# Inverse transforms of a Hyena group, split into even and odd tokens, with the halves of the spectrum summed and subtracted by GpSimd

## The reference, cut to what matters

```
v, x1, x2 = split(short_conv_centred(u))
z = x1 * fft_long_conv(v, k_freq[:, 0], skip[0])
z = x2 * fft_long_conv(z, k_freq[:, 1], skip[1])
return rmsnorm(z, norm_w)

def fft_long_conv(u, k_freq, d):          # u: (B, L, W), L = 256
    y = irfft(rfft(u, n=2 * L) * k_freq, n=2 * L)[:, :L]
    return y + u * d
```

## Time and profile before

| | us |
|---|---|
| median of 3 runs (1463.59 to 1465.66) | 1464.34 |
| the profiled execution's own time | 1464.21 |
| its span, first to last instruction | 1462.4 |
| TensorE busy in it | 1389.9 (95%) |
| GpSimd busy in it | 689.5 (47%) |

### The profile page before, as it was taken

One profiled execution on the slowest core, in us unless ns is written; L12 is line 12 of the kernel. 1 busy time (PEld: TensorE's weight loads), 2 busy tenths in 40 slices (PEclk: granted clock), 3 DMA queues, 4 the chain that ended last, 5 costly groups with the idle time before them and its releaser, 6 DMA issues.

```text
span 1462.4 us, 16428 instructions
## 1 busy us (share of the span) xinstructions
PE 1389.9 (95%) x6832; PEld 1098.3 (75%) x6832; DVE 462.2 (32%) x657; ACT 479.9 (33%) x730; POOL 689.5 (47%) x423
## 2 busy tenths in 40 slices
PE   5879999999899999999999899999989999999997
PEld 2567777787688877888876778777868888888885
DVE  3477754533302311000054677554250000000003
ACT  0764323323333222321247343312442322322212
POOL 0266544344455544544332756533625555555441
PEclk9989999999899999999999999999999999999999
DMA  4322111012333322333312211111213323323331
GB/s 172 105 61 70 44 44 44 30 52 78 117 94 98 91 85 87 115 97 90 101 46 84 72 44 56 38 38 44 72 62 97 102 88 99 101 95 112 96 96 77
DMA packets 31465, 116.82 MB, mean 80 GB/s; under 512 B 3488, under 2 KB 3616, under 8 KB 31136
## 3 DMA queue, kind: packets, MB, share of 16 engines
q1 hardware_dynamic: 31392, 115.78, 25.1%
HBM read 113.67 MB, written 2.10 MB: 79 GB/s over the span
## 4 chain that ended last, share of the span: by engine, by line
PE 83%; DVE 11%; ACT 3%; issue 1%; POOL 1%; DMA 0%; POOLq 0%; DVEq 0%; SPq 0%; ACTq 0%
PE ps L998 16%; PE ps L1000 15%; PE ps L999 15%; PE ps L1005 7%; PE ps L1006 7%; PE ps L1008 7%; PE ps L1195 4%; PE ps L1181 3%; PE ps L1118 2%; DVE amat L852 1%; PE ps L1045 1%; PE ps L1143 1%; DVE ring L836 1%; DVE cum L816 1%; POOL w_lo L641 1%
## 5 line engine op out<-in xcount | busy, mean ns | idle before, releaser
L641 POOL TENSOR_TENSOR w_lo<-w_raw,w_hi 128x1024 fp32r<-128x1024 f32 x198 | 475.1, 2400 | 533.0 <-ACT w_hi L362 533.0
L998 PE MATMUL ps<-h_hi,w_hi 128*128 128x512 f32 x1104 | 450.7, 408 | 3.1 <-POOL w_lo L641 1.6
L1000 PE MATMUL ps<-h_hi,w_lo 128*128 128x512 f32 x1104 | 433.2, 392 | 0.0
L999 PE MATMUL ps<-h_lo,w_hi 128*128 128x512 f32 x1104 | 432.9, 392 | 0.0
L362 ACT ACTIVATE w_hi<-w_raw 128x1024 fp32r<-128x1024 f32 x198 | 208.1, 1051 | 206.6 <-PE ps L1008 200.2
L998 PEld LDWEIGHTS ps<-h_hi,w_hi 128*128 128x128 f32 x1104 | 209.3, 190 | 54.2 <-issue 8.8
L999 PEld LDWEIGHTS ps<-h_lo,w_hi 128*128 128x128 f32 x1104 | 209.5, 190 | 47.7 <-issue 5.7
L1000 PEld LDWEIGHTS ps<-h_hi,w_lo 128*128 128x128 f32 x1104 | 209.0, 189 | 44.8
L976 DVE TENSOR_TENSOR hid<-ps,sg 128x512 f32<-128x512 f32 x44 | 30.4, 692 | 438.4 <-PE ps L1000 438.4
L1005 PE MATMUL ps<-w_hi,hid_hi 128*128 128x512 f32 x352 | 139.2, 395 | 1.8 <-POOL w_lo L641 1.8
L1006 PE MATMUL ps<-w_lo,hid_hi 128*128 128x512 f32 x352 | 138.9, 395 | 0.0
(11 more groups left out here) (140 smaller groups left out, 1434.5 us busy)
## 6 DMA issues: line engine op xcount, KB each, us to landing
w_raw<-in_units SPq DMA_DIRECT2D x198, 512.0 KB, 3.6
par<-in_par SPq DMA_DIRECT2D x2, 1310.5 KB, 6.3
gain<-in_gain SPq DMA_DIRECT2D x5, 512.0 KB, 4.7
x<-in_x SPq DMA_DIRECT2D x4, 512.0 KB, 10.0
out_y<-x SPq DMA_DIRECT2D x4, 512.0 KB, 2.6
cst<-in_cst SPq DMA_DIRECT2D x3, 512.0 KB, 6.6
mask_f<-in_mask SPq DMA_DIRECT2D x1, 640.0 KB, 5.5
cst<-in_cst SPq DMA_DIRECT2D x1, 224.0 KB, 2.7
```

Of the source, the lines that this page charges most:

```text
L641: nc.gpsimd.tensor_tensor(w_lo[:, g % RING], w_raw[:, g % RAW], w_hi[:, g % RING].bitcast(F32), ALU.subtract).then_inc(s_lo, 1)
L998: nc.tensor.matmul(out, hi, act_hi, start=start, stop=False)
L999: nc.tensor.matmul(out, hi, act_lo, start=False, stop=False)
L1000: return nc.tensor.matmul(out, lo, act_hi, start=False, stop=stop)
```

## The change

The upper half of the spectrum is stored in reversed order with its sine sign turned, so that frequency f and its mirror 255 - f have the same cosine at even tokens and opposite ones at odd tokens (and likewise for the sines). After the second `sums` of a convolution GpSimd does four more operations of 128x512 f32: two sums of the halves, written to prod, and two differences, written over the first half of spec. A new signal, `folded`, tells TensorE, which now waits for it in `back` where it waited for `yfd`. `back` makes even tokens from the sums and odd tokens from the differences, each with 2 components and 128 columns in place of 4 components and 256 columns. `gating` reads the even and odd halves of PSUM interleaved. The table inv shrinks from 4 x 256 to 4 x 128 columns, 512 KB to 256 KB, and ScalarE's `hyena_square(1)` loses its wait on `yfd`.

```diff
@@
-K_WIN = K_INV + 4 * SEQ
+K_WIN = K_INV + 4 * P
@@
+        even_odd = ((prod[:, 0], prod[:, 1]), (spec[:, 0], spec[:, 1]))
@@
+        folded = Signal(sem("s_folded"), 4)
@@ hyena_square
-                    act.wait_ge(yfd.sem, yfd.at(L, 8))
@@ sums
                 nc.gpsimd.tensor_tensor(im, im, prod[:, 1], ALU.add).then_inc(yfd.sem, 1)
+                if d:
+
+                    pool.wait_ge(yfd.sem, yfd.at(L, n + 1))
+                    for c in range(2):
+                        nc.gpsimd.tensor_tensor(even_odd[0][c], spec[:, c], spec[:, 2 + c], ALU.add)
+                    for c in range(2):
+                        last = nc.gpsimd.tensor_tensor(even_odd[1][c], spec[:, c], spec[:, 2 + c], ALU.subtract)
+                    last.then_inc(folded.sem, 1)
@@ gating
-                nc.vector.tensor_tensor(z, ps[:, 6 + b, :].rearrange("p (c t) -> p c t", c=2), z, ALU.mult)\
+                z = z.rearrange("p c (t e) -> p c t e", e=2)
+                nc.vector.tensor_tensor(z, ps[:, 6 + b, :].rearrange("p (c e t) -> p c t e", c=2, e=2), z, ALU.mult)\
@@ back
-                pe.wait_ge(yfd.sem, yfd.at(L, 2 * i + 2))
+                pe.wait_ge(folded.sem, folded.at(L, i + 1))
@@
                 for c in range(2):
-                    for f in range(COMPS):
-                        last = nc.tensor.matmul(ps[:, 6 + b, SEQ * c:SEQ * c + SEQ],
-                                                spec[:, f, P * (2 * b + c):P * (2 * b + c) + P], inv[:, f],
-                                                start=f == 0, stop=f == COMPS - 1)
+                    for e in range(2):
+                        for f in range(2):
+                            last = nc.tensor.matmul(ps[:, 6 + b, SEQ * c + P * e:SEQ * c + P * e + P],
+                                                    even_odd[e][f][:, P * (2 * b + c):P * (2 * b + c) + P],
+                                                    inv[:, 2 * e + f], start=f == 0, stop=f == 1)
@@ constants
-    dft = np.stack([np.cos(angle(f)), -np.sin(angle(f)), np.cos(angle(f + P)), -np.sin(angle(f + P))])
-    back = dft.transpose(0, 2, 1) * 2.0 / n
+    g = SEQ - 1 - f
+    dft = np.stack([np.cos(angle(f)), -np.sin(angle(f)), np.cos(angle(g)), np.sin(angle(g))])
+    back = np.stack([dft[c, e::2].T for e in range(2) for c in range(2)]) * 2.0 / n
```

## The result

The changed kernel takes 1472.7 us, median of 4 runs (1472.44 to 1474.32), against 1464.7 before: ratio 1.0058, interval 1.0042 to 1.0074. It is slower by 8.0 us, where 1462.6 was forecast, and lies outside the forecast range, which ended at 1469.5. The waits on which the forecast rested are there, nearly with the sizes worked out. What was wrong is how often the clock falls in them.

What follows compares the result with a forecast made beforehand. TensorE, busy 95% of the span, was taken to set the pace. 25.6 us saved, less 23.6 of stalls, plus 0.8 gives 2.8 gained, 1461.5; allowing for zero or one clock fall, 1462.6 us, range 1456 to 1469.5.

Steps and rivals of the forecast that it cites:

- The products saved: TensorE's 16 `back` calls, columns halved from 256 to 128: 1.6 us saved a call, 25.6 us in all.
- The fold's price: GpSimd's four added operations after each second `sums`: 5.0 us a fold, 40 us of GpSimd time in all.
- Slot 20: Third convolution: TensorE reaches `back` before the fold ends and stalls 3.9 us a layer.
- Slot 17: Second convolution: fold delays exponents, exp, w_hi and u copies, so TensorE's `turn_v` of head 3 stalls 3.5 us a layer.
- Slot 22: Fourth convolution: TensorE's `back` waits for the fold, slowed 0.45 us by VectorE; stall of 4.4 us a layer.
- The first convolution: Slots 12 to 14: earlier merging gains 1.1 us a layer, later exponents lose 0.7; no stall at `back`.
- The sum without the clock: Whole kernel: 25.6 us saved, 23.6 of stalls, 0.8 gained in the first convolution; 2.8 us gained.
- The clock in the stalls: Six new TensorE stalls: zero or one clock fall likeliest, 1461.5 or 1463.8 us, chance 0.55 with at most one.
- the rival: Clock falls at the new TensorE waits, 2.3 us each: three give 1468.4, six 1475.3; two or more, chance 0.16.
- Contention: Rival: added GpSimd work slows VectorE's SBUF operations, slots 12 to 17 and 22; 5 us more, 1466.5; chance 0.10.
- Hidden fold: Rival: TensorE comes to `back` after the fold, so the whole saving stays; 1436.5 us, chance 0.03.
- shorter stalls: Rival: faster folds or room in the exponents' chain shorten TensorE's stalls; 1454.5 or 1458.5 us, chance 0.16.

Runs made afterwards that it cites:

- exp_first: Changed kernel with the fold of slot 16 placed behind GpSimd's exponents instead of ahead of them; 1461.39 us, ratio 0.9978 to the kernel before.
- fill: Changed kernel with useless TensorE products, 12 a layer, put just before the new waits; 1460.08 us, ratio 0.9971 to the kernel before.
- late_back: Changed kernel with the inverse transforms of the third and fourth convolutions moved later; 1453.19 us, ratio 0.9922 to the kernel before.
- late_exp: Changed kernel with the edits of late_back and exp_first together; 1443.94 us, ratio 0.9852 to the kernel before.

## Why the prediction was wrong, by its own steps

- **The products saved.** 1.6 us a call forecast, 1.67 measured, and 26.4 us for all 16 with the clock held up. Right.
- **The fold's price.** 5.0 us forecast, 4.95 measured where GpSimd is alone. The estimate of 4.5 us from the Trainium skill (GPSIMD Engine Reference, section 3.1) is not borne out: the operations start 1.24 us apart and not 1.12.
- **The stalls.** Slot 20: 3.9 forecast, 3.73 measured. Slot 17: 3.5 and 3.40; `exp_first` shows the chain. Slot 22: 4.4 and 5.03; here contention was under-sized. I added 0.45 us once, but the broadcast multiplications of VectorE and GpSimd's fold slow each other as long as both run: the fold takes 6.2 us, and VectorE's four took 6.78 us where they had 4.63. With that the six are 24.3 us, against 23.6.
- **The first convolution.** 1.1 us a layer gained by short operations in place of w_lo, and a loss of 0.7: measured 1.1 and 0.4. Right in mechanism, and the loss smaller.
- **The sum without the clock.** 2.8 us gained was forecast, and -26.7 + 25.3 - 1.4 gives 2.8 us again. That it agrees to the tenth is luck: the saving was 1.1 us larger and the first convolution 0.6 us better, and the stalls took 1.7 us more.
- **The clock in the stalls.** This is the step that failed. The prediction said: "The other waits, up to 2.9 us, I read as too short for it", and "the trace shows it for one gap of 9.2 us only". Zero or one fall in six stalls was taken as likeliest, and there were five. Neither sentence is true of the trace of before. The earlier trace rows itself has a wait of 4.2 us beside the longest, since 13.4 us in two with 9.2 as the longest leave that much: it is the same wait in layer 1. Its end, the waits of 2.8 us at two norms, and the granted clock at these three places, all in the kernel before:

```profile
371.99 0.87 PE L1018 MATMUL ps<-cst,xs 128*128 128x128 f32 x4 [2.78 <-DVE xs L739]
807.29 1.23 PE L1088 MATMUL ps<-ring 64*128 64x128 f32 x8 [4.18 <-DVE ring L836]
1085.02 0.66 PE L1018 MATMUL ps<-cst,xs 128*128 128x128 f32 x4 [2.78 <-DVE xs L739]
```

```profile
372.00:374.00 2.00, 0.86 (x4) 0.46 (x4) 2.00 (x1) 1.14 (x3) 2.00 (x1) 0.57 0.00 0
806.00:808.00 2.00, 0.71 (x6) 0.71 (x8) 1.59 (x4) 0.63 (x1) 2.00 (x4) 0.50 0.67 219
1086.00:1088.00 2.00, 0.22 (x1) 0.23 (x2) 2.00 (x2) 0.31 (x1) 1.17 (x1) 0.50 0.00 0
```

Of the waits of 2.8 us and more with TensorE busy before them, four of five had ended in a fall: 9.2, 4.2, and two of the three at the norms. (Each of those two is followed within 0.9 us by another wait, of 1.9 and 2.1 us; the third, of 2.92 us, stands alone and left the clock up.) With these rows read, three or more falls in six stalls of 3.4 to 5.0 us was the likely case, and the sum of the rival, -2.8 + 5 x 2.3 = +8.7 us, is within 1 us of what was measured. I gave that rival, with two falls or more, 0.16.

- **The price of one fall.** 2.3 us forecast from the one, 2.1 measured as the mean of five (1.6 to 2.8). The size was right, and the count was not. The Trainium skill (TensorE: Matmul & The Clock Gate, section HAM oscillation) says that the cost is paid at each gap anew. The trace agrees for five of six, and `fill` shows that TensorE's idleness brings the cost and not the length of the wait: with the waits as long and filled, none of it is paid.
- **Contention.** 5 us more at TensorE through L835 and L836 did not come: the waits for merging fell to 3.3 us.
- **Hidden fold, shorter stalls.** Excluded by the measured waits.

Open is what decides whether a given gap ends in a fall. Two equal waits of 3.40 us, 716 us apart, went both ways, and so did two of 2.32 us in `late_back`, while both fell in `late_exp`; the norm's 2.92 us at 42 us left the clock up in the kernel before and not in the changed one. No run here varies a gap's length or place alone.

## What to carry to other kernels

When an edit moves a wait onto TensorE, read the granted clock in windows along the whole span before pricing the wait: here each wait of over 2 us cost its length and, more often than not, another 2 us behind it. A preparing step on another engine is priced by what stands behind it in that engine's list and by how soon its reader comes: the same fold cost nothing in one place, 3.4 us through a chain of three engines in another, and 5.0 us in the next. If such a wait can't be removed, work of no use put into it can be worth more than it costs.

## What the runs showed of the hardware that was not expected

- The clock can fall after the gap has ended: 0.5 us after work resumed in `late_back` and 1.5 us after in `late_exp`, both behind a gap of 2.32 us.
- TensorE came back to full clock 3.3 to 6.0 us after it resumed work, in five cases of one run.
- One execution ran at a granted clock of 0.95 from 22 us on, a level between the two, and took 1493.08 us where its kernel's others took 1486.3 to 1486.5.
- GpSimd's and VectorE's operations with both inputs in SBUF stretch each other: 1.6 us for a fold operation that takes 1.24 alone, and 1.7 for a VectorE multiplication that took 1.16 with fewer GpSimd operations beside it.
